# Delta rule of a two-block layer on one core: k's scalings moved to ScalarE, four of sixteen w products left out, the decay product of q in an earlier half, state copies ahead of the weights' rounding, k's turn one half later

## The reference

```
kb = k * beta[..., None]
A = einsum('bhnid,bhnjd->bhnij', kb, k) * decay * strict
T = triangular_solve(eye + A, eye)
u = einsum('bhnij,bhnjd->bhnid', T, v * beta[..., None])
w = einsum('bhnij,bhnjd->bhnid', T, kb * exp(gc)[..., None])
qk = einsum('bhnid,bhnjd->bhnij', q, k) * decay
q_dec = q * exp(gc)[..., None]
k_end = k * exp(g_last[..., None] - gc)[..., None]
def step(Sst, inp):                      # Sst starts as zeros
    v_new = u_n - einsum('bhid,bhde->bhie', w_n, Sst)
    o = einsum('bhid,bhde->bhie', qd_n, Sst) + einsum('bhij,bhje->bhie', qk_n, v_new)
    Sst = Sst * exp(gl_n)[..., None, None] + einsum('bhid,bhie->bhde', ke_n, v_new)
    return Sst, o
```

## Time and profile before

| | us |
|---|---|
| three runs | 2366.63, 2368.41, 2372.14 (median 2368.41) |
| the profiled execution | 2367.83 |
| its span | 2366.2 |
| PE busy (matmuls) | 2340.8 |
| DVE busy | 1627.0 |
| ACT busy | 1174.6 |
| POOL busy | 233.7 |
| mean granted clock of PE, share of full | 0.999 |

### The profile page before, as it was taken

The page is one execution under the profiler, slowest core; times in us unless marked ns, Lnnn a source line. Parts: engine busy times, 40 slices in busy tenths (PEclk is TensorE's granted clock), DMA queues, the critical chain, the costliest instruction groups (busy, mean ns, idle before and its releaser), DMA issues.

```text
span 2366.2 us, 35125 instructions
## 1 busy us (share of the span) xinstructions
PE 2340.8 (99%) x13692; PEld 1923.5 (81%) x13692; DVE 1627.0 (69%) x2147; ACT 1174.6 (50%) x1554; POOL 233.7 (10%) x410
## 2 busy tenths in 40 slices
PE   8999999999999999999999999999999999999998
PEld 7888888777777777788888888888888888888887
DVE  5899999878787878656665756666666544555565
ACT  5555555576454545444555654535353444443443
POOL 3000000112121213011000101001010000000100
PEclk9999999999999999999999999999999999999999
DMA  7566666766555658488655557776776755676673
GB/s 252 187 213 204 204 196 228 234 205 232 179 187 179 191 175 286 152 289 284 217 194 194 193 173 240 229 229 233 225 239 223 247 192 185 230 260 190 223 252 125
DMA packets 239247, 506.87 MB, mean 214 GB/s; under 512 B 15065, under 2 KB 15938, under 8 KB 238210
## 3 DMA queue, kind: packets, MB, share of 16 engines
q1 hardware_dynamic: 214898, 418.57, 53.8%
q0 software_dynamic: 24208, 86.31, 11.4%
HBM read 464.45 MB, written 40.39 MB: 213 GB/s over the span
## 4 chain that ended last, share of the span: by engine, by line
PE 65%; DVE 1%; DMA 1%; ACT 0%; issue 0%; POOL 0%; DVEq 0%; ACTq 0%
PE acc L2604 58%; PE acc L2624 2%; PE acc L2639 1%; PE aux L2666 1%; PE aux L2811 0%; DMA delta_branch_spill<-ol 0%; PE aux L3112 0%; DMA r1l<-delta_branch_spill 0%; PE aux L3117 0%; PE aux L3017 0%; PE aux L2652 0%; PE acc L3017 0%; PE aux L2917 0%; PE aux L2804 0%; PE aux L2904 0%
## 5 line engine op out<-in xcount | busy, mean ns | idle before, releaser
L1644 DVE TENSOR_TENSOR w_lo<-raw,w_hi 128x1024 fp32r<-128x1024 f32 x790 | 962.4, 1222 | 653.7 <-ACT w_hi L960 642.0
L960 ACT CAST w_hi<-raw 128x1024 fp32r<-128x1024 f32 x790 | 824.3, 1049 | 980.7 <-PE acc L2604 938.7
L2604 PE MATMUL acc<-w_hi,r1h 128*128 128x512 f32 x1828 | 722.3, 395 | 3.0 <-DVE w_lo L1644 1.9
L2604 PE MATMUL acc<-w_lo,r1h 128*128 128x512 f32 x1828 | 709.3, 388 | 0.0
L2604 PE MATMUL acc<-w_hi,r1l 128*128 128x512 f32 x1828 | 708.5, 388 | 0.0
L2604 PE MATMUL acc<-w_hi,r2h 128*128 128x512 f32 x1208 | 472.2, 391 | 0.2 <-DVE r2l L1738 0.2
L2604 PE MATMUL acc<-w_hi,r2l 128*128 128x512 f32 x1208 | 470.2, 389 | 0.0
L2604 PE MATMUL acc<-w_lo,r2h 128*128 128x512 f32 x1208 | 470.1, 389 | 0.0
L2604 PEld LDWEIGHTS acc<-w_hi,r1h 128*128 128x128 f32 x1828 | 343.3, 188 | 81.6 <-DVE w_lo L1644 6.3
L2604 PEld LDWEIGHTS acc<-w_hi,r1l 128*128 128x128 f32 x1828 | 343.3, 188 | 72.0
L2604 PEld LDWEIGHTS acc<-w_lo,r1h 128*128 128x128 f32 x1828 | 343.6, 188 | 65.4
(11 more groups left out here) (507 smaller groups left out, 1589.1 us busy)
## 6 DMA issues: line engine op xcount, KB each, us to landing
raw<-in_w_in SPq DMA_DIRECT2D x263, 1024.0 KB, 5.1
raw<-in_w_out SPq DMA_DIRECT2D x32, 1024.0 KB, 5.2
raw<-in_w_br_b SPq DMA_DIRECT2D x16, 1024.0 KB, 5.3
raw<-in_w_br_a SPq DMA_DIRECT2D x16, 1024.0 KB, 7.5
raw<-in_w_ple_gate SPq DMA_DIRECT2D x16, 1024.0 KB, 5.1
raw<-in_w_o_mla SPq DMA_DIRECT2D x16, 1024.0 KB, 5.1
raw<-in_w_o_conv SPq DMA_DIRECT2D x16, 1024.0 KB, 5.2
raw<-in_w_q_b SPq DMA_DIRECT2D x8, 1024.0 KB, 5.1
```

The costliest lines, as they stand in the source:

```text
L960: nc.scalar.copy(w_hi[:, h % HL, 0:n], raw[:, k % RAW, x * HALF:x * HALF + n]).then_inc(hi_ready, 1)
L1644: V.tensor_tensor(w_lo[:, h % HL, 0:n], raw[:, k % RAW, x * HALF:x * HALF + n], w_hi[:, h % HL, 0:n].bitcast(F32), ALU.subtract).then_inc( ...
L2604: ins = T.matmul(acc[:, s, x, 0:n], a[:, kt0 + k, xs_], w[:, h % HL, at], start=start and k == 0 and m == 0, stop=stop and k == kts - 1 an ...
```

## The change

It moves k's two scalings from DVE to ACT: `kbe` at half 3 (8 instructions; the first chunk's rows are left out), `ke` at half 5 (10 instructions; the last chunk's, which the scan does not use, are left out). PE computes no w for the first chunk (12 products in place of 16) and ACT's first copy of w is 256 columns wide in place of 512. `qdT` is made at half 11 for three chunks of four, in place of half 15. The last level's update of the inverse (half 15) and the state updates (halves 18, 20, 22) go from `delta` to `delta_first`, ahead of the rounding. k's own turn moves one half: unpacked 21, taps 21 to 23, silu 24, transposes 25; in pass 0 only the transposes move, 27 to 28.

```diff
-OWN = ((8, 0, 12, (12, 15), 15, 16), (16, 0, 20, (20, 22), 23, 24), (24, 0, 31, (27, 29), 30, 31))
-OWN_FIRST = ((8, 9, 10, (11, 15), 16, 19), (16, 20, 21, (22, 24), 25, 27), (24, 26, 27, (27, 29), 30, 31))
+OWN = ((8, 0, 12, (12, 15), 15, 16), (16, 0, 21, (21, 23), 24, 25), (24, 0, 31, (27, 29), 30, 31))
+OWN_FIRST = ((8, 9, 10, (11, 15), 16, 19), (16, 20, 21, (22, 24), 25, 28), (24, 26, 27, (27, 29), 30, 31))
@@ ACT, scan_operands
-                for n, r in enumerate(CHUNK_ROWS):
-                    act.wait_ge(sem("uw_done"), dv(4, TT + n + 1))
-                    sig(nc.scalar.copy(wT[:, :, :, r].rearrange("p t h i -> p (t h) i"), X[:, 2 + n].rearrange("p (m i) -> p m i", i=SEQ_CHUNK)),
-                        "w_ready", dv(2, n + 1))
+                act.wait_ge(sem("uw_done"), dv(4, TT + 1))
+                sig(nc.scalar.copy(wT[:, 1, :, CHUNK_ROWS[0]], X[:, 2, TOK:2 * TOK].rearrange("p (h i) -> p h i", i=SEQ_CHUNK)), "w_ready", dv(2, 1))
+                act.wait_ge(sem("uw_done"), dv(4, TT + 2))
+                sig(nc.scalar.copy(wT[:, :, :, CHUNK_ROWS[1]].rearrange("p t h i -> p (t h) i"), X[:, 3].rearrange("p (m i) -> p m i", i=SEQ_CHUNK)),
+                    "w_ready", dv(2, 2))
@@ ACT, delta
+                if hl == 3:
+                    act.wait_ge(sem("cols_ready"), dv(1, 1))
+                    for x, rows in ((0, CHUNK_ROWS[1]), (1, slice(0, P))):
+                        for h in range(GH):
+                            c.inc(A(kbe[rows, x, h], ktok[rows, x, h], ACT.Copy, scale=dcol[rows, 4, x, h:h + 1]))
+                if hl == 5:
+                    for x in range(TT):
+                        for dst, src, hs in PLACES:
+                            for h in range(hs.start, hs.stop):
+                                if x == 0:
+                                    c.inc(A(ke[dst, x, h], ktok[src, x, h], ACT.Copy, scale=dcol[src, 5, x, h:h + 1]))
+                                elif src.start == 0:
+                                    to = slice(dst.start, dst.start + SEQ_CHUNK)
+                                    c.inc(A(ke[to, x, h], ktok[CHUNK_ROWS[0], x, h], ACT.Copy, scale=dcol[CHUNK_ROWS[0], 5, x, h:h + 1]))
+                    c.wait()
+                    act.sem_inc(sem("k_scaled"), 1)
@@ DVE, delta_first (the block with hl == 18 + 2 * n moves here from delta, unchanged, ahead of the subtractions)
+                if hl == 5 + 2 * LEVELS:
+                    dve.wait_ge(sem("ly_done"), dv(LEVELS, LEVELS))
+                    for b in BLOCKS[::2]:
+                        ins = V.tensor_scalar(th(uinv)[b, :, LATE], blocks(0)[b], -1.0, None, ALU.mult)
...
@@ DVE, delta
-                if hl == 2:
-                    dve.wait_ge(sem("cols_ready"), dv(1, 1))
-                    c.inc(V.tensor_tensor(th(kbe), th(ktok), over(col(4), DK), ALU.mult))
-                if hl == 2:
-                    for dst, src, hs in PLACES:
...
                 if hl == 3:
+                    dve.wait_ge(sem("cols_ready"), dv(1, 1))
...
-                if hl == 15:
-                    dve.wait_ge(sem("egc_landed"), dv(32, 32))
-                    sig(V.tensor_tensor(flat(qdT), flat(qT), flat(egc_rep), ALU.mult), "qdT_ready", dv(1, 1))
...
+                if hl == 11:
+                    dve.wait_ge(sem("egc_landed"), dv(32, 32))
+                    sig(V.tensor_tensor(qdT[:, :, SEQ_CHUNK:], qT[:, :, SEQ_CHUNK:], egc_rep[:, :, SEQ_CHUNK:], ALU.mult), "qdT_ready", dv(1, 1))
@@ PE, delta, hl == 15
                     for m, (x, h) in enumerate(PAIRS):
                         for n, r in enumerate(CHUNK_ROWS):
+                            if (x, n) == (0, 0):
+                                continue
                             ins = T.matmul(X[:, 2 + n, m * SEQ_CHUNK:(m + 1) * SEQ_CHUNK], kbe[r, x, h], uinv[r, x, h], start=True, stop=True)
```

More of the change, by code:

```diff
@@ L2093, in delta @@
                             c.wait()
+                for n in range(1, NCH):
+                    x, (rows, out_rows) = n // 2, scan_rows(n)
+                    if hl == 17 + 2 * n:
+                        dve.wait_ge(sem("scan_done"), dv(SCAN, 2 * n))
+                        for h in (0, GH // 2):
+                            v = us[out_rows[h], x, h:h + GH // 2].rearrange("p h d -> p (h d)")
+                            ins = V.tensor_tensor(v, v, X[out_rows[h], 0, h * DK:(h + GH // 2) * DK], ALU.subtract)
+                            if h == 0:
+                                c.inc(ins)
+                        sig(ins, "scan_ready", dv(SCAN, 2 * n))
+                        c.wait()
@@ new lines, in delta_first @@
+                if hl == 4 + 2 * LEVELS:
+                    dve.wait_ge(sem("lx_done"), dv(LEVELS, LEVELS))
+                    sig(V.tensor_copy(xs_b, blocks(0)), "xs_ready", dv(LEVELS, LEVELS))
+                if hl == 5 + 2 * LEVELS:
+                    dve.wait_ge(sem("ly_done"), dv(LEVELS, LEVELS))
+                    for b in BLOCKS[::2]:
+                        ins = V.tensor_scalar(th(uinv)[b, :, LATE], blocks(0)[b], -1.0, None, ALU.mult)
+                        if b is BLOCKS[0]:
+                            c.inc(ins)
+                    sig(ins, "inv_ready", dv(LEVELS, LEVELS))
+                    c.wait()
```

112 lines of the change are left out of this document (42 added, 70 removed).

## The result

| | before | changed |
|---|---|---|
| median, us | 2368.24 (2366.63 to 2372.14, 9 runs) | 2374.97 (2371.08 to 2381.65, 9 runs) |
| profiled execution, us | 2367.83 | 2371.08 |
| its span, us | 2366.2 | 2369.4 |

The ratio is 1.0029, 95% interval [1.0021, 1.0037]: the change makes the kernel 0.3% slower. The profiled execution of the changed kernel is the fastest of its nine runs, so its profile shows the loss at its mildest: 3.2 us of span where the medians are 6.7 apart. The runs also scatter over 10 us, those of before over 5.5. Three of the nine stand at 2371.1 to 2371.6 with a mean granted clock of 0.999, the other six at 2374.2 to 2381.7 with 0.998 or 0.997. A clock lower by 0.001 over the whole execution is 2.4 us (an estimate from 2370 us), so the slower runs lose time of that size to the clock alone. The loss and the scatter both have to be explained.

The account below looks back on a forecast made before the run. PE was taken as the bound, busy 2340.8 of 2366.2 us, with only its waits and small matmuls reducible. 1.1 + 4.7 + 0.8 - 2.2 gave 4.4 to 4.5 us less, from 2368.41 to 2363.9; range 2360.0 to 2369.4.

Parts of the forecast that it names:

- k's turn in pass 0: k's transposes at the end of pass 0: a half put in between fills the 1.40 us wait; gain 1.1 us (0 to 1.4).
- The way to q's transposes: Waits at u and q's transposes shrink by earlier qdT and shorter w: 1.47 in passes 1 and 3, 1.31, 0.48; sum 4.7.
- The w term: w products on PE: four of 16 left out save 0.12 us each, 0.48 together per pass.
- Rival 2: w products: leaving them out saves nothing, as row halves run side by side; 3.4 gained, not 4.7; 2365.2; chance 0.15.
- 0.12 each is then the price of half a pair: Argument at the w products against Rival 2: a pair would take 0.24 us, twice what one takes alone.
- State updates ahead of rounding: State product of line 2904: its operand comes some 2 us sooner, so two waits go; gain 0.8 us (0 to 0.9).
- k's scalings on ScalarE: Ten scalings in half 5 delay the next cast and `xs` at half 6: cost 0.56 us a pass, 2.2 in four.
- The bound of the sum: Upper bound on the `xs` cost at half 6: 6 us (1.49 a pass) if each scaling takes its full 0.388.
- if the ten scalings take over 3.5 us: Sign that the forecast is wrong, at half 5's ke scalings on ACT, which were forecast to take 3.04 us.
- v's turn through POOL and its DMAs is used only at half 31, seven halves on.: v's evacuation on ACT goes about 2 us later relative to PE; its turn is used only at half 31; no cost counted.
- Rival 3: Scalings on ACT in halves 3 and 5 cost more, 0.5 each; `xs` 12.1 us late in four passes; 2373.9; chance 0.06.
- The range: Whole kernel: 2360.0 (no new wait, full 1.4, 1 us scatter) to 2369.4 (scalings at 0.388, w worth nothing, 1 us scatter).

Follow-up runs that it names:

- r3: Kernel before with q's decay product moved to half 11, k's turn one half later and the conv branch's last reload ahead of the store: 2362.72 us, ratio 0.9980.
- s4: r3 with the state and inverse updates ahead of the roundings: 2362.60 us, ratio 0.9980.
- t1: r3 without the first chunk's w, a second copy of the second chunk's products standing in its place: 2368.25 us, ratio 1.0007.
- p3: Kernel before with only the state copies and updates and the last inverse level ahead of the roundings on VectorE: 2372.85 us, ratio 1.0019.
- e1: Changed kernel with the conv branch's last reload issued ahead of the store of pass 2's output: 2370.78 us, ratio 1.0014.
- e3: e1 with k's scalings back on VectorE at half 2, as in the kernel before: 2366.09 us, ratio 0.9997.
- p1: Kernel before with only k's scalings moved to ScalarE (kbe at half 3, ke at half 5): 2373.97 us, ratio 1.0024.
- p4: Kernel before with only k's turn one half later: 2369.53 us, ratio 1.0009.
- s2: Changed kernel with the first chunk's w computed again (kbe on all rows, the wide copy): 2370.00 us, ratio 1.0012.
- e2: Kernel before with the conv branch's last reload issued ahead of the store of pass 2's output: 2367.34 us, ratio 0.9999.
- r2: Kernel before with extra column work on GpSimd in the last pass, ahead of the conv branch's reloads: 2374.92 us, ratio 1.0026.
- r1: Changed kernel with k's turn back at its old half: 2375.42 us, ratio 1.0033.

## Why the prediction was wrong

- **k's turn in pass 0.** Forecast 1.1, the table shows 1.02. Right.
- **The way to q's transposes.** Forecast 4.7; the steps at u and q are 0.54 + 0.78 in pass 1, 0.77 in pass 2 and 0.58 + 0.92 in pass 3, or 3.6. The mechanism held: the waits are gone. That those at u hang on the update of the inverse is confirmed, too: they stay in r3 (1.1 us) and are gone in s4, which adds the updates first. The size was off by its w term, above all in pass 2 and in the last pass.
- **The w term.** Forecast 0.12 for each of four products, 0.48 a pass. Measured 1.93 to 1.92 a pass: nil. Rival 2, with a chance of 0.15, was right, and the rule of the Trainium skill (TensorE: Matmul & The Clock Gate, Part 3) that it rested on agrees with t1's 0.88 for the same number on one side. I argued against it from "0.12 each is then the price of half a pair", and that is what it was. No term had the loss that goes with leaving w out, 1.7 to 4.2 us in four pairs.
- **State updates ahead of rounding.** Forecast 0.8; the changed kernel has 0.68 and 0.30. But p3 shows that this gain exists only together with k's later turn, which I costed apart.
- **k's scalings on ScalarE.** The wait on `xs`, its place and its chain are as forecast; the size was not. Forecast 0.56 a pass from a pitch of 0.295 us; the ke scalings stand 0.35 apart on average, for they change partitions after every second one, and 0.19 goes between the last and the cast. Measured 1.17 a pass, 4.7 in four (the fourth is seen in e1) instead of 2.2. The bound of the sum, 1.49 a pass at 0.388 each, does not come out of its own chain either: ten then take 0.84 more than 3.04, which makes 0.56 + 0.84 = 1.40. What would show the forecast wrong was "if the ten scalings take over 3.5 us": they took 3.57.
- **The step that failed.** "v's turn through POOL and its DMAs is used only at half 31, seven halves on." The reload of the conv branch was put at nothing, and the last pass was to gain 0.48 on w and lose 0.56 on `xs`; its half 6 lost 4.2. I followed GpSimd's queue for what the turn sends through it, and not for what stands behind it in the last pass: a store, a wait for its landing, and a reload with 1.0 us to spare. The forecast also took TensorE's lead as pure gain, though each microsecond of lead is a microsecond less for a transfer whose time hangs on something else. That term cost 2.54 us of wait and 1.6 of lower clock behind it.
- **Rival 3**, slower at 2373.9, came near the time by another way: the scalings in half 5 did cost more, but not 0.49 each.
- **The range**, 2360.0 to 2369.4, does not follow from the terms beside it: they give 2360.5 (6.9 us gained, 1 of scatter) and 2370.1 (0.7 lost, 1 of scatter). Neither end reaches the 2374.97 measured.

Against the forecast of 4.5 us faster: the q and w terms gave 1.1 less, the scalings cost 2.5 more, the reload 3.0 (its 4.2 less the wait on `xs` under it), and `tinv`, late by q's pad, 1.2 (0.20 and 0.95). That is 7.8, where the forecast and the changed kernel's profiled execution (3.2 over that of before) are 7.7 apart. The sum is closer than it deserves, since differences outside it cancel: 0.8 gained before the first step of the change, 0.6 at 1050 to 1111 us, and 1.1 lost near 1590 us behind the late store. The other 3.5 us up to the median are the scatter, in whose runs the granted clock is 0.997 or 0.998 instead of 0.999. A fall of the clock cost 1.7 us in the traces, so two or three more of them a run would do (an estimate); no such run of the changed kernel has a trace. e3's trace is of its slowest run (2371.8, clock 0.998) and has two such falls, behind the stalls of 1.75 and 1.49 us inside small matmuls, so these are one way to it.

## What to carry to other kernels

When an edit makes the bounding engine run ahead, list every transfer that it will meet, with its time to spare, also three passes later, and follow each queue past the moved step to its next wait for a landing. Judge a move between engines by the half it is put in before the engine: the same scalings cost four waits of 1.1 us in one half, 6.4 us by the medians, and none of them two halves on. Where parts of a change meet on one queue, their prices don't add: p1 to p4 alone sum to 11.5 us slower, while the whole change, with w left out besides, is 6.7 slower. Run them alone and together.

## What was not expected of the hardware

- A stop of TensorE can be paid for twice. Behind stops of 1.49 and 1.75 us (e3), 1.67 (s2), 2.18 (p4), 2.37 (e2, on `w_lo`, at 1112 us) and 2.54 (changed kernel) the granted clock was 0.83 over the 10 us in which it fell, which is 1.7 us more. Behind 5.55 us it was 0.50, the lower level, for a whole 5 us (r2). The length of the stop alone does not decide it: behind 1.69 (r3, at 1047 us), 1.73 (r1, at 731 us) and another 1.75 us (e3, at 1589 us) it stayed at 1.00.
- Leaving out matmuls that cost no time, since they ran beside others, went with 1.7 to 4.2 us more in four pairs of kernels, with more scatter, and with a store 450 us later that took about twice as long to land.
- TensorE can stop for 1.4 to 1.8 us inside a run of matmuls that wait for nothing. All 13 stops of this kind ended 1.3 to 1.6 us behind a 16 KB packet of the instruction queue.
- GpSimd's column instructions of 0.2 us take 1.2 beside a rounding on VectorE (913.31 and 916.98 in the changed kernel), and whether they meet one changes with a shift of about a microsecond.
